# One trunk layer on one core: sample queries inside the attention loop, sample memory scores inside the memory loop, and identity turns ahead of each wait

## Time and profile before

| | us |
|---|---|
| three timed runs | 1992.2, 1996.03, 2000.11 |
| profiled execution | 1989.02 |
| its span, first to last instruction | 1987.2 |

### The profile page before, as it was taken

The page is one execution under the profiler, slowest core; times in us unless marked ns, Lnnn a source line. Parts: engine busy times, 40 slices in busy tenths (PEclk is TensorE's granted clock), DMA queues, the critical chain, the costliest instruction groups (busy, mean ns, idle before and its releaser), DMA issues.

```text
span 1987.2 us, 34900 instructions
## 1 busy us (share of the span) xinstructions
PE 1879.4 (95%) x15062; PEld 1609.8 (81%) x15062; DVE 1210.6 (61%) x1579; ACT 568.4 (29%) x962; POOL 544.8 (27%) x384
## 2 busy tenths in 40 slices
PE   7999999997899799999998789999999999999999
PEld 6988888884566344448997569999999999999998
DVE  5485673665676888875433635785387167375475
ACT  5322221353544355452121422211011011021026
POOL 2211221340000144423224013333333333333530
PEclk9999999998999899999999989999999999999999
DMA  7211211132000688853124301111111110211202
GB/s 235 54 45 33 55 45 32 40 80 103 1 1 20 270 328 332 320 196 121 32 86 144 113 25 59 43 42 44 54 53 34 57 49 28 69 38 38 81 26 88
DMA packets 161141, 174.64 MB, mean 88 GB/s; under 512 B 21846, under 2 KB 146796, under 8 KB 156604
## 3 DMA queue, kind: packets, MB, share of 16 engines
q1 hardware_dynamic: 145072, 91.43, 15.5%
q0 software_dynamic: 7168, 75.50, 10.0%
q10 hardware_dynamic: 8750, 5.49, 0.9%
HBM read 159.24 MB, written 13.25 MB: 87 GB/s over the span
## 4 chain that ended last, share of the span: by engine, by line
PE 84%; DVE 9%; ACT 3%; issue 2%; DMA 1%; POOL 1%; SPq 0%; ACTq 0%; DVEq 0%; POOLq 0%
PE PS L754 20%; PE PS L756 19%; PE PS L755 19%; PE PS L1039 4%; PE PS L791 4%; PE PS L1072 3%; PE PS L986 2%; PE PS L835 2%; PE PS L964 2%; PE PS L1029 2%; PE PS L1054 1%; DVE Sst L1900 1%; DVE small L2087 1%; PE PS L942 1%; PE PS L1242 1%
## 5 line engine op out<-in xcount | busy, mean ns | idle before, releaser
L700 POOL CAST whi<-wraw 128x1024 fp32r<-128x1024 f32 (+4 forms) x142 | 140.1, 986 | 1025.0 <-PE PS L756 905.9
L754 PE MATMUL PS<-BH,whi 128*128 128x344 f32 x1152 | 369.7, 321 | 3.7 <-DVE cu L1832 3.7
L755 PE MATMUL PS<-BL,whi 128*128 128x344 f32 x1152 | 367.8, 319 | 0.0
L756 PE MATMUL PS<-BH,wlo 128*128 128x344 f32 x1152 | 367.6, 319 | 0.0
L702 POOL TENSOR_TENSOR wlo<-wraw,whi 128x1024 fp32r<-128x1024 f32 (+4 forms) x142 | 306.7, 2160 | 11.4
L754 PEld LDWEIGHTS PS<-BH,whi 128*128 128x128 f32 x1152 | 216.7, 188 | 4.5 <-DVE cu L1832 4.0
L755 PEld LDWEIGHTS PS<-BL,whi 128*128 128x128 f32 x1152 | 216.8, 188 | 0.5 <-issue 0.5
L756 PEld LDWEIGHTS PS<-BH,wlo 128*128 128x128 f32 x1152 | 216.8, 188 | 0.0
L754 PE MATMUL PS<-XH,whi 128*128 128x344 f32 x528 | 179.8, 340 | 3.1 <-DVE XL L1787 3.1
L755 PE MATMUL PS<-XL,whi 128*128 128x344 f32 x528 | 169.0, 320 | 0.0
L756 PE MATMUL PS<-XH,wlo 128*128 128x344 f32 x528 | 168.9, 320 | 0.0
(11 more groups left out here) (445 smaller groups left out, 3716.3 us busy)
## 6 DMA issues: line engine op xcount, KB each, us to landing
wraw<-in_w_up_dram SPq DMA_DIRECT2D x44, 512.0 KB, 3.7
wraw<-in_w_in_dram SPq DMA_DIRECT2D x20, 512.0 KB, 4.0
wraw<-in_w_down_dram SPq DMA_DIRECT2D x24, 256.0 KB, 2.8
wraw<-in_w_down_dram SPq DMA_DIRECT2D x16, 320.0 KB, 3.2
xt_kept<-XT SPq DMA_DIRECT2D x1, 4128.0 KB, 12.6
XT<-xt_kept SPq DMA_DIRECT2D x1, 4128.0 KB, 14.0
xstage<-in_x_prompt_dram SPq DMA_DIRECT2D x8, 512.0 KB, 10.2
wraw<-in_w_out_dram SPq DMA_DIRECT2D x8, 512.0 KB, 4.3
```

The lines of the kernel that those rows point to most:

```text
L700: gp.tensor_copy(hi, raw).then_inc(w_hi_done, 1)
L754: pe.matmul(out, wh[:, t, 0:m], hi[:, tile(t), s], start=(t == first), stop=False)
L755: pe.matmul(out, wh[:, t, 0:m], low, start=False, stop=False)
L756: ins = pe.matmul(out, wl[:, t, 0:m], hi[:, tile(t), s], start=False, stop=(t == last))
```

## The change

1. `latent_queries(n)`: the turns of `w_uk` go behind units 8 to 11 of prompt attention, `qlat` behind unit 15, `snew` and `ckvn` behind unit 19. DVE's copies go to units 9, 11, 13, 15 to 18 (four of the sixteen in each) and 20; ACT's to units 8 and 10. `wukT`, `qlatR`, `qlat`, `qr` and one page piece buffer get other places in memory. The clearing of the four banks, the turned rope keys and three of the four page pieces of group 0 stand ahead of the wait for the last values.
2. The samples' queries go to DRAM (`q_kept`, 8 x 512) and come back as eight broadcasts `QB` of 128 x 512; the one-hot product and its tile go. SP waits for both in the queue described above. The samples' products stand at units 2, 3, 4 and 6 to 10 (`sample_at`); `sct` stands at unit 11, the softmax at 12, `spt` at 13, `spv` at 14.
3. The values of a unit, its high and its low part are made one unit later (`memory_values(n - 1)`, `memory_high`, `memory_low`).
4. `keep_busy`: 6 turns of the identity matrix (3 from unit 11 on, none at 14 and 15) into bank 7, which nobody reads, ahead of each wait for `m_new`: 11 x 6 + 3 x 3 = 75.
5. Feed-forward: `b` is taken out ahead of ACT's seed for f = 0 to 4, not for f = 0 alone.

```diff
+            if 8 <= n < 12:
+                use(("wk", n - 8), [(1, 3, 5, 1)[n - 8]], "sv"[n % 2])
+            elif n == 15:
+                use("qlat", [3], "v")
+            elif n == 19:
+                use("snew", [1], "v")
+                use("ckvn", [5], "v")
...
+        sample_at = {2: 0, 3: 1, 4: 2, 6: 3, 7: 4, 8: 5, 9: 6, 10: 7}
...
+                    for b in range(2):
+                        sp.dma_start(sK[b][:, :, :], i["cache_mem_k"][0, b].rearrange("(t p) h e -> p t (h e)", p=P)).then_inc(sk_in[b], 16)
+                    sp.wait_ge(qs_set, 1)
+                    sp.dma_start(q_kept, QS[0:NS, :]).then_inc(q_out, 16)
+                    sp.wait_ge(q_out, 16)
+                    for b in range(NS):
+                        sp.dma_start(QB[b][:, :], q_kept[b:b + 1, :].broadcast_to([P, ME])).then_inc(q_in, 16)
...
+            def keep_busy(b, count):
+                for r in range(count):
+                    pe.transpose(PS[:, b, P * (r % 3):P * (r % 3) + P], ident[:, :], ident[:, :])
...
+            for n in range(len(munits)):
+                if n < 14:
+                    keep_busy(7, 6 if n < 11 else 3)
+                pe.wait_ge(m_new, n + 1)
+                turn(("mpt", n), [Pm[n % 2][:, hh, m * P:m * P + P] for hh in range(2) for m in range(2)])
+                if n + 2 < len(munits):
+                    memory_scores(n + 2)
+                if n:
+                    memory_values(n - 1)
...
             memory_scale(0)
-            for n, (q, hp) in enumerate(munits):
+            for n in range(len(munits)):
                 if n + 1 < len(munits):
                     memory_scale(n + 1)
                 if n + 2 < len(munits):
                     memory_max(n + 2)
+                if n:
+                    memory_low(n - 1)
+                if n in sample_at:
+                    b = sample_at[n]
+                    ve.wait_ge(q_in, 16 * NS)
                     ve.wait_ge(sk_in[b % 2], 16 * (b // 2 + 1))
...
+            emptied(ve, ("S", units[-1]))
+            ve.memset(PS[:, 0:4, :], 0.0).then_inc(part_zero, 1)
             turn_rope_keys(0)
-            for n in range(4):
+            for n in range(3):
                 turn_key_pair(0, n)
+            full(ve, ("po", NT - 1, H // 2 - 1))
+            ve.tensor_reduce(sel32[:, :], ident[:, :].rearrange("p (j h) -> p h j", j=4), AX, ALU.add)
+            turn_key_pair(0, 3)
...
-                if f == 0:
+                if f in FPARTS[0]:
                     scaled(("b", f), RB2[:, :], RB1[:, :])
```

More of the change, by code:

```diff
@@ L198, in build_program @@
         PTm, sK = [PTm0, PTm1], [sK0, sK1]
+        QB = place(S0, A0, *[(f"QB{n}", [P, ME], F32) for n in range(NS)])
         acth, actl, ab, ct, cu = place(A0, A1, ("acth", [P, FSLOTS, TT], F32R), ("actl", [P, FSLOTS, TT], F32R),
@@ L1000, in _ @@
                     attention_values(n, u)
[L1003 to L1021, removed]
+                latent_queries(n)
             def part_scores(g):
@@ L1187, in _ @@
                 end(ins)
[L1188 to L1192, removed]
-            pe.wait_ge(prod_done, NS)
-            begin("sct")
-            for m in range(2):
-                ins = pe.transpose(bank("sct")[0:32, m * P:m * P + P], sc[:, m, :], ident[:, :])
-            end(ins)
-            pe.wait_ge(s_new2, 1)
@@ L1199, in _ @@
-            turn("spt", [scr[0:32, m * P:m * P + P] for m in range(2)])
-            emptied(pe, "spt")
-            pe.wait_ge(sv_in, 16 * NS)
-            begin("spv")
-            for m in range(2):
-                for b in range(NS):
-                    r = 32 * (b % 4)
-                    ins = pe.matmul(PS[r:r + 32, uses["spv"][1][b // 4], :], pm[:, m, :], sV[b][:, m, :],
-                                    start=(m == 0), stop=(m == 1), skip_group_check=True)
-            end(ins)
+            memory_scores(0)
@@ new lines, in _ @@
+            memory_scores(1)
+            emptied(pe, ("mko", 1))
+            for n in range(len(munits)):
[7 more added lines that the diff above has]
+                    memory_values(n - 1)
+                if n == 11:
+                    pe.wait_ge(prod_done, NS)
+                    begin("sct")
+                    for m in range(2):
+                        ins = pe.transpose(bank("sct")[0:32, m * P:m * P + P], sc[:, m, :], ident[:, :])
+                    end(ins)
+                elif n == 13:
+                    pe.wait_ge(s_new2, 1)
+                    turn("spt", [scr[0:32, m * P:m * P + P] for m in range(2)])
+                elif n == 14:
+                    emptied(pe, "spt")
+                    pe.wait_ge(sv_in, 16 * NS)
+                    begin("spv")
+                    for m in range(2):
+                        for b in range(NS):
+                            r = 32 * (b % 4)
+                            ins = pe.matmul(PS[r:r + 32, uses["spv"][1][b // 4], :], pm[:, m, :], sV[b][:, m, :],
+                                            start=(m == 0), stop=(m == 1), skip_group_check=True)
+                    end(ins)
@@ L1639, in _, with memory_high @@
             memory_exp(1)
-            for n, (q, hp) in enumerate(munits):
+            def memory_high(n):
+                q, hp = munits[n]
+                full(act, ("mpo", n))
+                act.activation(omh[:, 2 * hp:2 * hp + 2, q * P:q * P + P], bank(("mpo", n))[:, 0:2 * P].rearrange("p (h q) -> p h q", h=2),
+                               ACT.Copy).then_inc(om_hi, 1)
+            for n in range(len(munits)):
                 if n >= 2:
@@ L2302, in _ @@
+            memory_low(len(munits) - 1)
+            full(ve, "spo")
             ve.wait_ge(om_hi, len(munits) + 1)
```

198 lines of the change are left out of this document (113 added, 85 removed).

## The result

| | before | changed |
|---|---|---|
| median of the timed runs, us | 1996.8 (4 runs, 1992.2 to 2000.1) | 1977.5 (4 runs, 1975.3 to 1979.5) |
| ratio to before | | 0.9905, interval 0.9886 to 0.9924 |
| profiled execution, its span | 1989.0, 1987.2 | 1975.3, 1973.4 |
| mean granted clock | 0.983 | 0.985 |

What follows compares the result with a forecast made beforehand. The tensor engine, 84% of the chain, was taken to bound the kernel, with gains only where it stalls or runs at half clock. 10.7 + 8.7 + 1.7 + 5.4 = 26.5 us off the 1996.0 median gave 1969, range 1956 to 1986.

Steps and rivals of the forecast that it cites:

- part 5: Feed-forward: early `b` removes PE's 3.7 us wait at tile 1 and 1.7 us of half clock, 5.4 us gained.
- Part 1: Sample queries inside prompt attention: page scores start 17.6 us earlier, the loop grows by 6.9 us, 10.7 us gained.
- The page loads: Rival: pages come late, by up to 13 us at group 2, leaving a gain of 13.5 us; chance 0.06.
- Parts 2 to 4: Memory attention: the loop keeps its pace and 1.36 us wait, only its ends change, 8.7 us gained.
- the rival of the half eaten gain: Prompt attention's loop grows by 12 us and memory attention's clock dips stay, leaving 16.5 us gained, 1979.5 us; chance 0.18.
- The round trip: Rival: DVE in memory attention waits for the queries' eight broadcasts from DRAM, 14.5 us slower, 2010.5 us; chance 0.05.
- The dip at `w_mo`: Start of the product with `w_mo`: 4 us at clock 0.57 lose 1.7 us, counted as gained.
- The turns: 75 identity products in memory attention cost nothing and hold the clock of `spv`, `spo` and the start of `w_mo`.
- The rival on this: Memory attention: the clock falls despite the turns or would have held without them; at most 5 us, no separate chance.

Runs made afterwards that it cites:

- the faster loop: Changed kernel with ACT making unit n - 1's high part ahead of the exponentials of unit n + 2 in memory attention (high part first): 1992.8 us, 0.9852 of before.
- late `b`: Changed kernel with `b` taken out early for feed-forward tile 0 alone, as before the change: 2004.0 us, 0.9902 of the kernel before.
- part 5 alone: Kernel before with only `b` taken out early for feed-forward tiles 0 to 4: 2023.7 us, 1.0008 of the kernel before.
- the changed kernel again: Changed kernel without any edit, measured once more as the measure for the experiments: 2008.5 us, 0.9924 of the kernel before.

## Why the prediction was right, and where not

The direction and the cause of the gain were right. The size was missed by 8.5 us in the median (1977.5 for 1969), by 12.7 in the profiled execution (13.8 gained for 26.5, with 3.4 of the 12.7 ahead of all that was changed) and by 10.3 in the experiments (16.2 for 26.5). In the profile and in the experiments, where the parts can be told apart, part 5 is about two thirds of it.

- **Part 1, predicted -10.7:** -8.9 in the profile, -7.9 alone. The step at `qlat` was right: 3.23 us of standing and 1.18 of copies, where the sum had 3.7 and 1.2. The gap closed by 16.7 for 17.6. The loop grew by 7.9 for 6.9. That microsecond is less than executions differ: in the experiments' traces the loop with part 1 takes 186.1 to 188.4 us. The clock reads 0.95 over it where the earlier trace rows had 0.97, but it reads 0.95 in the experiments without part 1 as well (178.7 and 178.9 us). Splitting it further was not tried.
- **The page loads** were not late: the page stage is 220.2 for 220.8. That rival fell.
- **Parts 2 to 4, predicted -8.7:** -9.3 in the profile, -8.2 to -9.5 alone. The loop kept its pace and the 1.36 wait, as said, and `spv` took 3.64 for 3.8. (Its price at half clock in the prediction, 6.8, should have been twice the 3.6 of full clock, 7.2; only the rival of the half eaten gain uses it.) The reason given for the wait (ACT's order, not PE) was put to the test by moving one step in that order, and the wait went with it.
- **The round trip** held nothing up; that rival fell, with about 1 us of room: the first sample product of the changed kernel starts 13.6 us behind the first memory scores. In the faster loop DVE does wait 0.57 us for it, and there the broadcasts have landed 12.6 us behind the first memory scores and 12.1 us behind the issue of the write, where the prediction's estimate by the Trainium skill had 8.8 (the section that it names is on DMAs that GpSimd issues, and these are SP's). Two sentences of the prediction on it misread the page of the profile: its part 6 does show a DMA that writes DRAM and is read back (`xt_kept`, 4128 KB, 12.6 and 14.0 us), and not every read of 512 KB or more lands at over 100 GB/s (`xstage` from `x_prompt` 512 KB in 10.2 us, 51 GB/s).
- **The dip at `w_mo`, predicted -1.7:** the term came out (-1.5) by luck, and its reason did not. The clock there is 1.00 in the first profile of the changed kernel, and `a` of tile 1 is taken out 89.6 us behind the start of `w_mo`, where before it was 91.1. But the same kernel in the experiments has the dip (0.58 in the first 4 us, and 91.1), and the kernel without turns has none (1.00). Over all traces, three of the eight with turns and one of the six without have no dip. The turns do not decide it, and what does stays open.
- **The turns** were costed at nothing, and no cost of them can be told. What they were said to give, the clock of the tail, did not come from them: `spv` takes 3.64 us and `spo` 1.85 in all eleven traces that have part 2, the three without turns included, and the stage is at 0.91 with them and at 0.94 without. The rival on this, which could be true beside the forecast, was true as far as the traces go.
- **Part 5, predicted -5.4, is the step that failed.** It read: "DVE stands still for 3.42 us ahead of ACT's seed, and the taking out of `b` (1.23) fits in. ... Both go: 5.4 us." The first half is right: the idle went from 3.42 to 2.36. But the step assumed that DVE then has that time left over. It hasn't. It lies behind POOL's subtraction: the last product grows to 3.32, and from the taking out of `a` in tile 1 to that of `b` in tile 5 the changed kernel takes 105.7 us in both of its traces, where late `b` takes 103.9. So DVE is 1.8 us later although it idles less, and PE is 5.5 earlier (3.7 of stall and some 1.8 of clock). They meet at tile 5, where `b` is late again, with 6.6 us of wait. Behind that wait the rest of the feed-forward part takes 1.2 us longer (from `b` of tile 5 to the last `actl` 571.2 for 570.0), at a clock of 0.74 in the stretch. 1.8 + 1.2 = 3.0, which is what the trace of part 5 alone shows. 5.4 forecast and 3.0 the other way make 8.4 us. That this is so near to the 8.5 missed in the median is partly chance: in the medians of the experiments part 5 alone missed by 6.7 (+1.3 for -5.4), part 1 by 2.8 and parts 2 to 4 with their dip by 0.8.

The rows to see it by stood in the trace of before: the convolution's two products of 8 columns take 2.63 us in tile 1 and 0.48 in tile 2, and the copy of 10 columns, 0.17 in those two tiles, takes 2.11 in tile 3. DVE first:

```profile
1263.95 2.63 DVE L2311 SCALAR_TENSOR_TENSOR ct<-sconv,convc,ct 128x8 f32<-128x8 f32 x2
...
1285.74 0.48 DVE L2311 SCALAR_TENSOR_TENSOR ct<-sconv,convc,ct 128x8 f32<-128x8 f32 x2
...
1302.97 2.11 DVE L2315 COPY atail<-ab 128x10 f32<-128x10 f32 x1
```
```profile
1263.03 3.26 POOL L702 TENSOR_TENSOR wlo<-wraw,whi 128x1024 fp32r<-128x1024 f32 x1
...
1302.65 2.40 POOL L702 TENSOR_TENSOR wlo<-wraw,whi 128x1024 fp32r<-128x1024 f32 x1
```

The Trainium skill, "SBUF — State Buffer", section "Who interferes with whom", says that a DVE instruction with two SBUF inputs contends with a GpSimd instruction that reads SBUF, that the port pair they share is locked by one of them at a time, with the order of issue deciding who blocks, and that a DVE instruction with at most one SBUF input does not contend outside DVE's 2-port modes. By that rule the trace agrees: the products of two SBUF tensors stretch to 3.3 us, and the taking out of `b` (one input in PSUM) is 1.22 or 1.23 in all these kernels. The copy of 10 columns has one SBUF input and stretches all the same; whether it runs in a 2-port mode no run shows. So moving the taking out of `b` changed only which other steps meet POOL.

## What to carry to other kernels

Idle time of an engine ahead of a step is room only if the engine's other steps keep their length when they move. Where one instruction shows two durations, as the two small products do with 0.48 and 2.63 here, find what runs beside the long one before counting on the idle. A stall that is taken away also brings the engine that waited earlier to the next join: walk the schedule on to the place where the old order comes back, here tile 5. And when a wait is said to be due to the order of steps on one engine, look whether the change at hand makes it possible to swap them: that was worth as much as all the rest (15.7 us against 14.5).

## What the runs showed of the hardware

- DVE's products of two SBUF tensors of 1032 columns take 1.23 us alone and up to 3.32 in the changed kernel where they meet POOL's subtraction of two SBUF tensors (3.45 in the kernel with `b` early for all tiles). POOL's subtraction of 1024 columns takes 2.38 to 2.42 where no such product is under way at its start and 3.23 to 3.44 where one is (26 and 18 times in the kernel before, from the product with `w_mo` on). With POOL's cut to 8 columns, DVE's read 1.23 to 1.29 in those tiles.
- DVE's copy of 10 columns within SBUF takes 0.17 us where it does not meet POOL's subtraction and 0.56 to 2.32 where it does. DVE's products with one input in PSUM take 1.22 or 1.23 also where they meet it (45 times in the same part of the kernel before).
- The granted clock falls to half without long waits: PE's waits in memory attention are at most 2.1 us in the kernel before, and the stage reads 0.88. In the changed kernel they are under 4 us, and it reads 0.91 with 384 matmuls in 79.3 us and, without the turns, 0.94 with 309 in 78.8. Turns of the identity did not raise it there.
- Whether the clock is at half at a given place can differ between executions with the same instructions up to there (0.58, 1.00 and 1.00 at the start of `w_mo` for the changed kernel again, late `b` and early `b` for all tiles, on one chip), worth 1.5 us. A term of that size can't be predicted from one profile.
- 16 KB (8 rows of 2 KB) written to DRAM and read back as eight broadcasts of 256 KB had landed 12.6 us after the first memory scores and 12.1 after the issue of the write, in the kernel with the high part first.
- The same kernel took 1996.8 us in the measurement of the result and 2022.4 to 2023.0 us on three chips in the experiments; from the first to the last `pieces` copy it is 220.8 in the one and 248.7 to 251.5 in the traces of the others. Why is not shown.
